# Router sums taken from the raw rows, with the norm's scale and shift folded into the router weights, and the product with the reciprocal root moved to GpSimd

## The reference, cut to what matters

```
h = rmsnorm(x, norm_ffn_g[l]) * (1 + scale) + shift      # scale, shift: one vector per token group
g_prob = softmax(t @ w_grp)                              # t = h, 4 groups, take the best
e_logits = t @ w_exp                                     # 4 experts per group, take the best two
y = sum of the two experts' SwiGLU outputs, gated
x = x + gate * y
```

## Time and profile before

| what | value |
|---|---|
| median of 3 runs | 801.81 us (800.67, 801.81, 805.41) |
| the profiled execution: its time, its span | 803.29 us, 801.5 us |
| PE busy, share of the span | 94% |
| DVE, ACT, POOL busy | 29%, 21%, 6% |
| HBM traffic | 367 GB/s over the span |
| mean granted TensorE clock | 0.962 of full speed |

### The profile page before, as it was taken

One profiled execution on the slowest core, in us unless ns is written; L12 is line 12 of the kernel. 1 busy time (PEld: TensorE's weight loads), 2 busy tenths in 40 slices (PEclk: granted clock), 3 DMA queues, 4 the chain that ended last, 5 costly groups with the idle time before them and its releaser, 6 DMA issues.

```text
span 801.5 us, 10420 instructions
## 1 busy us (share of the span) xinstructions
PE 757.1 (94%) x4039; PEld 424.2 (53%) x4039; DVE 234.2 (29%) x665; ACT 165.1 (21%) x372; POOL 50.1 (6%) x74
## 2 busy tenths in 40 slices
PE   5899979999999999999989999999999899999996
PEld 4388448773444344434468866876333434333444
DVE  2300440442111111110389953153212111211115
ACT  3020231341000100010330775243011001000003
POOL 5014000001000000000100000000100000101100
PEclk9799999979999999999999999977999899999997
DMA  9996999988999999999998258657999996999971
GB/s 301 400 397 234 395 409 427 384 322 350 427 427 427 424 428 427 425 427 428 395 402 343 121 212 352 277 210 284 419 426 430 421 428 278 366 428 423 418 309 56
DMA packets 43506, 289.66 MB, mean 361 GB/s; under 512 B 4513, under 2 KB 5997, under 8 KB 30386
## 3 DMA queue, kind: packets, MB, share of 16 engines
q1 hardware_dynamic: 37616, 275.78, 84.2%
q0 software_dynamic: 5056, 11.98, 4.0%
q10 hardware_dynamic: 770, 1.06, 0.4%
HBM read 285.63 MB, written 8.52 MB: 367 GB/s over the span
## 4 chain that ended last, share of the span: by engine, by line
PE 83%; DMA 9%; DVE 3%; issue 2%; ACT 1%; POOL 1%; PEld 0%; SPq 0%; DVEq 0%; PEldq 0%; POOLq 0%
PE ps L531 79%; DMA ring<-in_w_ada 6%; DMA ring<-in_conv_w 4%; DVE work L1954 1%; PE ps L1113 1%; PE ps L761 1%; PE ps L834 1%; PE ps L802 0%; PE ps L683 0%; DVE rstd L1691 0%; POOL work L1572 0%; DVE back L2205 0%; PE ps L1233 0%; ACT back L1306 0%; PEld ps L531 0%
## 5 line engine op out<-in xcount | busy, mean ns | idle before, releaser
L531 PE MATMUL ps<-ring,work 128*64 128x512 f32 x1088 | 304.1, 595 | 0.6 <-ACT work L1400 0.3
L531 PEld LDWEIGHTS ps<-ring,work 128*64 128x64 f32 x1088 | 93.9, 137 | 143.4 <-issue 142.7
L531 PE MATMUL ps<-back,ring 128*128 128x256 f32 x656 | 146.8, 384 | 4.3 <-ACT back L1306 3.1
L531 PEld LDWEIGHTS ps<-back,ring 128*128 128x128 f32 x656 | 124.3, 192 | 25.8 <-issue 5.4
L531 PE MATMUL ps<-bench,work 128*64 128x512 f32 x208 | 93.1, 596 | 0.3 <-DMA spare<-in_moe_w 0.3
L531 PE MATMUL ps<-spare,work 128*64 128x512 f32 x176 | 77.6, 594 | 0.0
L531 PE MATMUL ps<-back,work 128*64 128x512 f32 x160 | 72.0, 596 | 0.0
L1954 DVE TENSOR_TENSOR work<-work,ps 128x256 f32<-128x256 f32 x34 | 19.5, 615 | 142.3 <-PE ps L531 142.1
L531 PE MATMUL ps<-ring,csil 128*32 128x512 f32 x352 | 45.6, 649 | 6.0 <-DMA ring<-in_w_ada 6.0
L2169 DVE SCALAR_TENSOR_TENSOR work<-work,dw 128x256 f32<-128x256 f32 x120 | 50.8, 477 | 1.0
L1372 ACT ACTIVATE work<-ps 128x512 f32<-128x512 f32 x15 | 9.0, 597 | 179.4 <-PE ps L531 179.4
(11 more groups left out here) (247 smaller groups left out, 639.7 us busy)
## 6 DMA issues: line engine op xcount, KB each, us to landing
ring<-in_moe_w SPq DMA_DIRECT2D x60, 2048.0 KB, 18.8
ring<-in_w_ada SPq DMA_DIRECT2D x22, 2048.0 KB, 18.2
bench<-in_moe_w SPq DMA_DIRECT2D x11, 2048.0 KB, 18.4
spare<-in_moe_w SPq DMA_DIRECT2D x10, 2048.0 KB, 20.3
back<-in_moe_w SPq DMA_DIRECT2D x9, 2048.0 KB, 18.5
ring<-in_conv_w SPq DMA_DIRECT2D x6, 2048.0 KB, 25.8
ring<-in_moe_w SPq DMA_DIRECT2D x6, 1024.0 KB, 29.7
ring<-in_w_in_ab SPq DMA_DIRECT2D x2, 2048.0 KB, 26.0
```

What stands on the lines that cost most here:

```text
L531: return nc.tensor.matmul(out, lhsT, rhs, start=start, stop=stop, skip_group_check=True)
```

## The change

The router's products read `xT` in place of `hT`, with weights `wg` = router weight times gain, made per token group by three DVE instructions in `weigh_route` while DVE waits for the mixer's last product. The term of the shift is one product of a matrix of ones with `wshift`, the sum over k of router weight times shift, on which the other products accumulate. The first half of the router's products is put ahead of the second half of the column sums, the second half at the top of `moe`, ahead of the modulation tiles. Two products with one-element operands turn the root from a row into a column per token; DVE takes its reciprocal and forms the logits in `route`. The 16 DVE instructions of the norm are replaced by 8 on POOL (`norm_rows`, x times reciprocal, 128x256 each), and ACT's instruction that added the shift now also multiplies by the gain. The transposes of h go chunk by chunk and come after the modulation tiles; `ada_turn` comes behind them; the copies of the transposed banks follow in the order 0, 2, 1, 3.

```diff
+            def logits(l, start, stop):
+
+                pe.wait_ge(wg_ready, l + 1)
+                for k in range(start, stop):
+                    if k == 0:
+                        mm(ps_shift, ones[:, :], wshift[:, :, :])
+                    for g in range(2):
+                        mm(ps_logit[:, g, :], xT[:, k, g * TG:(g + 1) * TG], wg[:, k, g, :], False, k == DC - 1)
...
+            logits(0, 0, DC // 2)
             norm_sums(1, DC // 2)
...
             def moe(l, n):
 
+                logits(l, DC // 2, DC)
+                pe.wait_ge(root_ready, n + 1)
+                for g in range(2):
+                    last = mm(ps_root[:, g:g + 1], root[0:1, g * TG:(g + 1) * TG], ones[0:1, 0:1], False, True)
+                last.then_inc(route_done, 1)
                 pe.wait_ge(mod_taken, (4, 8)[l])
                 for j in range(len(ADA_ROOT[l])):
                     ada_rows(ADA_ROOT[l], j)
...
                 for k in range(DC):
                     pe.wait_ge(h_ready, DC * n + k + 1)
                     for g in range(2):
-                        last = mm(ps_logit[:, g, 0:20], hT[:, k, g * TG:(g + 1) * TG],
-                                  wr[:, l, k, :], k == 0, k == DC - 1)
-                last.then_inc(route_done, 1)
-                ada_turn(ADA_ROOT[l])
-
-                for g in range(2):
-                    for k in range(DC):
                         last = nc.tensor.transpose(ps[:, 2 * g + k // 4, (k % 4) * P:(k % 4 + 1) * P],
                                                    hT[:, k, g * TG:(g + 1) * TG], ident)
                         if k % 4 == 3:
                             last.then_inc(htok_done, 1)
+                ada_turn(ADA_ROOT[l])
                 pe.wait_ge(mask_ready, l + 1)
...
+            logits(1, 0, DC // 2)
             norm_sums(3, DC // 2)
...
                         last = nc.scalar.activation(hT[:, k, g * TG:(g + 1) * TG], hT[:, k, g * TG:(g + 1) * TG],
-                                                    ACT.Identity, bias=mod[:, shift[0], shift[1] + k, g:g + 1])
+                                                    ACT.Identity, bias=mod[:, shift[0], shift[1] + k, g:g + 1],
+                                                    scale=gain[:, shift[0], 1, k, g:g + 1] if n % 2 else 1.0)
...
+            def norm_rows(l):
+
+                pool.wait_ge(rstd_ready, l + 1)
+                for k in range(DC):
+                    nc.gpsimd.tensor_tensor(hT[:, k, :], xT[:, k, :], rstd[:, :], ALU.mult).then_inc(hpre_ready, 1)
...
+            def weigh_route(l):
+
+                shape = [P, DC, 2, 20]
+                w = wr[:, l].unsqueeze(2).to_broadcast(shape)
+                link(V.tensor_tensor(wg[:, :, :, :], w, mod[:, l, 24:32, :].unsqueeze(3).to_broadcast(shape), ALU.mult))
+                link(V.tensor_reduce(wshift[:, :, :], wg[:, :, :, :].rearrange("p k g e -> p g e k"), AX.X, ALU.add))
+                V.tensor_tensor(wg[:, :, :, :], w, gain[:, l, 1].unsqueeze(3).to_broadcast(shape), ALU.mult).then_inc(wg_ready, 1)
+
+            def norm_moe(n):
+
+                dve.wait_ge(root_ready, n + 1)
+                V.reciprocal(rstd[:, :], root[:, :]).then_inc(rstd_ready, 1)
...
+            weigh_route(0)
             residual(1, psx, 0, 2, lambda k: product(dve, y_done[0], "out", 0, k))
-            norm_dve(1, lambda k, g: gain[:, 0, 1, k, g:g + 1])
+            norm_moe(1)
...
             def route(l):
                 dve.wait_ge(route_done, l + 1)
-                link(V.tensor_copy(lg[:, :, :], ps_logit[:, :, 0:20]))
+                V.tensor_copy(wshift[:, :, :], ps_shift)
+                link(V.reciprocal(rtok[:, :], ps_root))
+                for g in range(2):
+                    last = V.scalar_tensor_tensor(out=lg[:, g, :], in0=ps_logit[:, g, :], scalar=rtok[:, g:g + 1],
+                                                  in1=wshift[:, g, :], op0=ALU.mult, op1=ALU.add)
+                link(last)
...
             take_mod(1, 2, 4)
+            weigh_route(1)
             residual(3, sq, 1, 2, lambda k: dve.wait_ge(yb_ready, k + 1))
-            norm_dve(3, lambda k, g: gain[:, 1, 1, k, g:g + 1])
+            norm_moe(3)
```

More of the change, by code:

```diff
@@ L163, in backbone @@
         ps_rank = ps[:, 5, NT + 64:NT + 112].rearrange("p (s e) -> p s e", s=3)
-        ps_logit = ps[:, 4:6, NT:NT + 32]
+        ps_logit = ps[:, 4, NT:NT + 40].rearrange("p (g e) -> p g e", g=2)
+        ps_shift = ps[:, 4, NT + 40:NT + 80].rearrange("p (g e) -> p g e", g=2)
+        ps_root = ps[:, 4, NT + 80:NT + 82]
         ring = sb("ring", [P, SLOTS, DC * TW])
@@ L257, in backbone @@
         lg = sb("lg", [P, 2, 20])
+        wg = sb("wg", [P, DC, 2, 20])
+        wshift = sb("wshift", [P, 2, 20])
+        rtok = sb("rtok", [P, 2])
         r1 = sb("r1", [P, 2, 16])
@@ L351, in backbone @@
         route_done = sem("route_done")
+        wg_ready = sem("wg_ready")
+        rstd_ready = sem("rstd_ready")
         gexp_in = sem("gexp_in")
@@ L1463, in moe_act @@
                     act.wait_ge(s_zero, 16)
-                for b in range(4):
-                    act.wait_ge(htok_done, 4 * l + b + 1)
+                for n, b in enumerate((0, 2, 1, 3)):
+                    act.wait_ge(htok_done, 4 * l + n + 1)
                     rows = slice((b % 2) * 64, (b % 2 + 1) * 64)
@@ L1469, in moe_act @@
                                          ACT.Copy).then_inc(htok_ready, 1)
-                for b in range(4):
-                    act.wait_ge(htok_ready, 4 * l + b + 1)
+                for n, b in enumerate((0, 2, 1, 3)):
+                    act.wait_ge(htok_ready, 4 * l + n + 1)
                     last = nc.scalar.activation(ps[:, b, :], cst[:, 0:512], ACT.Copy, scale=0.0)
@@ L1625, in send_rows @@
                                              bounds_check=ROWS - 1, oob_is_err=False).then_inc(y_sent, 16)
+            def norm_rows(l):
+                pool.wait_ge(rstd_ready, l + 1)
+                for k in range(DC):
+                    nc.gpsimd.tensor_tensor(hT[:, k, :], xT[:, k, :], rstd[:, :], ALU.mult).then_inc(hpre_ready, 1)
             def fetch_rows(l):
                 for g in range(2):
-                    pool.wait_ge(htok_ready, 4 * l + 2 * g + 2)
+                    pool.wait_ge(htok_ready, 4 * l + g + 3)
                     pool.dma_start(hbuf[l][g * TG:(g + 1) * TG, :], htok[:, g, :]).then_inc(h_stored, 16)
@@ L1641, in fetch_rows @@
                         send_rows(i - 2)
+            norm_rows(0)
             fetch_rows(0)
@@ L1655, in _ @@
             pool.wait_ge(s_zero, 16)
+            norm_rows(1)
             fetch_rows(1)
```

## The result

The changed kernel takes 815.92 us (median of four runs, 814.4 to 818.42), the kernel before 801.46 beside it (800.67 to 805.41): a ratio of 1.0169, 95% interval 1.0136 to 1.0201. Forecast were 799.0 us and 795 to 804, with 0.05 on slower by over 1%. The profiled execution took 815.69 us with a span of 812.8; the span of before was 801.5, so 11.3 us are to be found. (The medians differ by 14.5: the profiled execution of before was 1.8 us above its median, and the changed kernel's time lies 2.9 us above its span, where before it was 1.8.)

A forecast was written before the change was run, and what follows sets the result against it. PE bounds the kernel, with 83% of the span, chiefly at the two expert entries. Gains of 0.2 us in layer 0 and 2.6 in layer 1 sum to 2.8, taking the median 801.81 to 799.0 us; range 795 to 804.

The forecast's parts named there:

- It passes on: End of layer 0: its 0.2 us gain survives the weight stream, since expert tiles are issued as PE frees their slots.
- a sign of being wrong: First expert products starting over 2 us earlier in layer 0, or later than before in layer 1, would refute the forecast.
- The entries: The stretches leading into the experts: gains of 0.2 us in layer 0 and 2.6 us in layer 1.
- the gather: Layer 0, behind the ranks and DVE's gap of 1.53 us: expected at 169.85 against 170.01 before.
- the turning of the modulation rows: PE in layer 0, after ACT's copy of the modulation rows: expected to take 1.85 us, ending at 167.05.
- h was complete: Layer 0, with ACT setting the pace: last chunk of h expected at 164.6, against 160.94 before.
- The scale operand: ACT's 16 instructions making h: 0.11 us more each, from 0.30 to 0.41, within bounds of zero to 0.2.
- rival 2: Clock falls early, in the first batch of small router products; sums and tiles take twice as long: 811.2 us, chance 0.12.
- Rival 1: POOL's 8 products each make one DVE router instruction wait 0.684 us; mask 5.5 us later, total 801.3 us, chance 0.25.
- the 4 to 6 foretold: Sign for the forecast: the router's mask ready 4 to 6 us earlier, without PE profiting.
- Taking it earlier gains nothing by itself: Router's decision at the expert entries is already hidden under PE's work; only shorter PE and ACT queues gain.

The follow-up runs named there:

- e2: Changed kernel, with SP issuing the weight tile that goes into h's place only after POOL has issued both token-row stores: 810.34 us, ratio 1.0074 to the kernel before.
- e1: Changed kernel with 20 empty semaphore increments on DVE, putting its later code back in its old place: 805.82 us, ratio 1.0029 to the kernel before.
- e10: Changed kernel with four empty increments on DVE ahead of the wait for the convolution's mean: 806.81 us, ratio 1.0024 to the kernel before.
- e4: Kernel before with 108 empty increments at DVE's start, placing its layer 1 code as in the changed kernel: 813.34 us, ratio 1.0109.
- e11: Changed kernel with two empty increments on DVE ahead of the wait for the convolution's mean: 813.74 us, ratio 1.0133 to the kernel before, two runs only.
- e7: Kernel before with one edit alone, the tile for h's place issued behind POOL's second store: 803.20 us, ratio 0.9996.
- e3: Changed kernel with both DVE's 20 empty increments and the stores ahead of the tiles: 797.43 us, ratio 0.9913 to the kernel before.
- e9: Changed kernel with the stores ahead of the tiles and the 8 products on DVE instead of POOL, no empty increments: 797.15 us, ratio 0.9931 to the kernel before.
- e8: Kernel before with stores first, POOL's products and ACT's gain and shift, router in the old order, increments replacing DVE's 16 instructions: 805.81 us, ratio 1.0044.
- e5: e3 with the 8 products of x and reciprocal on DVE instead of POOL, and two increments in place of ten: 796.71 us, ratio 0.9905 to the kernel before.
- e6: Changed kernel's router and PE order with the stores first, but h made as before by 16 DVE instructions: 800.30 us, ratio 0.9960 to the kernel before.

## Why the prediction was wrong

**The step that failed** stands at the end of layer 0: "It passes on: ... its expert tiles are issued as PE frees their slots (183.56), so it moves along." The tiles did move along, 1 us earlier (182.59). The fetch on POOL's queue did not: it moved 2 us the other way, and the two met. The order 0, 2, 1, 3 of ACT's copies makes both groups complete only with the last two copies, so POOL's two stores moved too, from either side of a weight tile to beside it. The prediction listed the copies for ACT's time and for the exponentials, and never followed what is issued behind them. It cost 7.6 us where it arose; with e2's edit the end comes 5.6 us earlier by the medians (815.92 to 810.34), 7.6 by the ratios to the before of each group. It also made layer 1's first expert product later than before (554.14 against 551.31), which the prediction had named as a sign of being wrong; the entry itself had got shorter.

**The term that was missing** is the place of DVE's code: 8.7 us, shown from both sides (e1 and e10 take it away, e4 makes it without the change, e11 moves it by two instructions). DVE's program got 10 instructions shorter per layer, and the sum counted only what those instructions took. Nothing in the rows could have given the price; a bound was there all the same: the trace of before has gaps of 5.92 and 4.67 us in DVE's sequencer at the jump into the crowded pair (623 to 635), where they are hidden: the changed kernel has one only there, 5.47 us, and from the fetch indices ahead of that jump to the next takes 59.62 us against 59.87. The Trainium skill, "Runtime: NRT & Kernel Launch", section "Instruction fetch mechanics", says that a taken branch to code outside the loaded window makes the engine fetch it first, and gives blocks of 16 KiB, 256 instructions. The traces agree on the first, with a packet of the instruction queue in either gap (689.7, 695.0), but not on the size: here these packets are of 8 KB, and 108 instructions forward (e4) put DVE's code where 20 backward do, that is, the places repeat after 128.

**Right, with its size, in layer 0 by luck.** The entries: forecast 0.2 and 2.6 us, measured 0.8 and 2.3. Each is the difference of two single traces; over all traces here the entry of layer 0 takes 23.84 to 26.10 us with the old order on PE and 22.08 to 24.18 with the new one. In layer 0 the gather came 1.8 us before its forecast (168.03 against 169.85), because the turning of the modulation rows ran at 2.4 GHz, 1.06 us instead of the 1.85 taken from the earlier trace rows, and h was complete at 163.77 instead of 164.6. Of the 2.0 us by which the gather came earlier than before, 1.0 were lost again up to the first expert product: the gather itself took 3.75 us instead of 2.87, with the clock at the lower level from 166.75 to 173.58. That 0.8 lies so near to 0.2 is luck. The scale operand costs ACT 0.09 us per instruction (6.26 / 16 against 4.78 / 16), forecast 0.11. The clock stays at 1.00 through the modulation tiles, so rival 2, the only one on the slower side, did not happen; the loss came from elsewhere.

**Right in number, open in cause.** Layer 1's entry is largely a matter of the clock. Windows of 20 us: the kernel before, the changed kernel, then e7 (the old order on PE):

```profile
532.00:552.00 20.00, 18.47 (x95) 17.86 (x96) 10.27 (x53) 10.64 (x22) 1.10 (x2) 0.57 0.68 265
```

```profile
532.00:552.00 20.00, 17.10 (x108) 13.22 (x106) 12.99 (x48) 13.25 (x30) 6.68 (x10) 0.76 0.77 292
```

```profile
532.00:552.00 20.00, 18.26 (x108) 17.13 (x110) 11.99 (x59) 12.14 (x28) 1.10 (x2) 0.74 0.69 261
```

e7's entry takes 24.32 us, hardly more than the changed kernel's 24.06, without any of the change: the clock happened to come back sooner. Both stand at the lower level for 10.2 us in this entry, the kernel before for 17.1; where that time is 6.8 us (e2, e3, e9, e10), the entry takes 22.4 to 22.7. What holds in every run is where the clock falls: 7.7 to 8.4 us after the last update of x with the old order on PE (the kernel before, e4, e7, e8), 11.8 to 14.7 us with the new one. That the new order gains at e3's level (some 6 us against the kernel before, by the ratio 7.0) is measured; how much of it is PE's shorter queue and how much the clock was not separated.

**Rival 1** was right as a mechanism and wrong in its price. Six of the router's instructions with two SBUF operands take 0.47 to 0.71 us beside POOL's products, against 0.17 to 0.19 without them (e5), while the reductions stay at 0.16. That agrees with the Trainium skill, "SBUF — State Buffer", section "SBUF: two separate sides", by which such an instruction and a GpSimd product lock each other out. The price was wrong because not each of the eight products holds up an instruction: the chain grows by 2.7 us, not by 5.5, so that the mask is ready 2.2 us earlier and not the 4 to 6 foretold, and nobody waits for it.

**"Taking it earlier gains nothing by itself"** holds for the old order on PE only. With the transposes moved ahead the ranks are asked for sooner, and then DVE's 16 products make the mask 2.2 us late (e6). The two halves of the change need each other: alone, the router gains 3.2 us and the product loses 3.5 (both by their ratios to the kernel before), where both together gain 7.0 (e3). What the second half has to bring is eight products in place of 16, with the gain on ACT; on which engine the eight stand makes no difference that can be told (e5).

## What to carry to other kernels

When a copy or a semaphore moves, follow every transfer that is issued behind it, on POOL's queue as well as SP's, and compare its moment with the issue of the large transfers around it: a small indirect fetch 0.3 us ahead of 4 MB took 11.6 us, one 3.3 us ahead 4.4. In a kernel with jumps, a change in the number of instructions is a change in itself: look for gaps of an engine's sequencer behind jumps that no semaphore explains, and before judging an edit, put the code back in its place with empty increments.

## What the runs showed of the hardware

- The instruction queue that DVE's gaps go with moves packets of 8 KB, and the places of DVE's code repeat after 128 instructions (e4). Behind a jump a gap takes 4.6 to 6.0 us, and a block across the end of a piece pays twice (5.86 and 4.73 us; four instructions further on, none).
- A 512 KB store issued beside two 2 MB tiles lands after 10 to 15 us; one issued 1.4 us ahead of them after 3.1. The first indirect fetch of a layer took, when it left at least 0.96 us ahead of the next tile, 3.3 to 4.5 us; when it left between 0.55 us ahead and 0.09 behind, 10.4 to 11.6.
- Behind a wait of 4.6 us in the middle of dense products PE's clock stood at the lower level for the next 6.8 us, and 2.5 us were lost beyond the wait.
- A GpSimd product that reads SBUF stretched DVE instructions with two SBUF operands beside it from 0.17 to some 0.66 us each: six of them in each layer, 2.7 us in all in layer 0.
